# Down-projection of four FFN tiles: one product of 8 x 22 weight blocks, or seven products of half tiles

## The chip, the cores and the metric

The kernel runs as one program on all 8 cores of one Trainium2 chip, two dies of four cores. Each core handles one prompt sequence (2048 tokens and 16 meta tokens) and 16 of the 128 sample tokens. There is no exchange between cores. The metric is the device time in microseconds (us) of the slowest core, as a median over runs.

Names of engines: TensorE is PE in the profile (its weight loads are PEld), VectorE is DVE, ScalarE is ACT, GpSimd is POOL, SyncE is SP. SP and POOL issue the DMAs. SBUF is the on-chip memory, PSUM the accumulators that PE writes: 8 banks of 512 fp32 columns.

## The reference, cut to what matters

```python
def trunk_layer(x, ...):                       # x: (B, T, 1024)
    h = rmsnorm(x, g_pre_mix); z = h @ w_in    # token mixer: pooling and short convolution, two gates
    ...
    x = x + rmsnorm(merged @ w_o, g_post_mix)
    h = rmsnorm(x, g_pre_ffn)
    upc, new_ffn = causal_dwconv(h @ w_up, buf_ffn, w_ffn_conv)   # (B, T, 2*2816), width 3
    gate, val = jnp.split(upc, 2, axis=-1)
    y = (jax.nn.silu(gate) * val) @ w_down                        # (B, T, 2816) @ (2816, 1024)
    x = x + rmsnorm(y, g_post_ffn)
```

The outputs are the rows after the layer and the last rows of the pooling, convolution and FFN inputs, for prompts and samples. The change touches the product with w_down.

## The kernel before

The work is feature-major: a tile is 128 channels (partitions) by up to 512 tokens, and products are PE matmuls with a 128x128 weight block as the stationary operand and N tokens as the moving one, in bf16, summed in a PSUM bank.

The 2080 tokens go through two phases. The mixer phase has 5 tiles (512 tokens, then 392 four times). In each, `F_block` makes 16 input projections with pooling and convolution on DVE, `B` makes the gates and the merge, `WO` the output projection, and `epi` the norms, the residual (x is added by a POOL-issued DMA that accumulates into SBUF) and the FFN input, which goes through DRAM (`h2T`). The FFN phase has 5 tiles of `TB_N` = 448, 456, 448, 456 and 256 tokens. In each, `pair(t, j)` for j = 0 to 21 makes one gate and one value chunk of 128 channels: 2 x 8 matmuls into two PSUM banks, a copy with the first convolution tap on ACT (L879), two more taps for both on DVE (L883, four instructions), silu on ACT (L896), and the product on POOL (L897) into row j of the gated activation G (22 rows of N tokens, bf16).

`wdown(t, m)` is the down-projection of tile t for 128 output channels m = 0 to 7: 22 matmuls of N columns in one bank, one per row of G. ACT then writes the result to Y, scaled (L914), and its square to YSQ (L917). The eight of tile t stand between the pairs of tile t+1, at the positions of `WD`, `WD1` and `WDL`. `epi_y(t)` sums the squares, has PE add them over the channels (one f32r matmul), takes the reciprocal root on ACT, scales Y on DVE (L931, four instructions of two rows each) and sends it with an accumulating POOL DMA onto the residual in `yT`. For the fourth tile POOL adds the residual itself (L936), in the last microseconds, and SP stores. The fifth tile's down-projection, `down_last`, is token-major: G is stationary, the weights move, in 66 matmuls of 512 and 44 of 256 columns; DVE and ACT normalize (L987, L982, L1000, L1002, L1006), SP stores `y_last`.

The fp32 weights w_dn are cast to bf16 by POOL DMAs during tiles 0 and 1 of the FFN (`wdn_load`), kept in DRAM as `w_dnb` and loaded again for each later tile: one load of 704 KB per m, into a ring of 4 buffers. A load is issued once the product that used its buffer is done. The last tile's weights need four more buffers.

Nothing is ordered by hand inside an engine but PE: `Sched` takes the operations in program order, keeps PE's order except for a few floating ones (the f32r sums), and lists the others by readiness and priority in its own model (`order`). Each engine then works strictly down its list, waiting for semaphores; a waiting instruction holds all behind it. The seven PSUM banks 0 to 6 are given out in turn (`next_bank`), so a matmul group also waits until ACT and DVE are done with what stood in its bank seven groups before.

## Time and profile before

| | |
|---|---|
| Median of 3 runs | 807.48 us (806.51 to 807.51) |
| Span of the profiled execution, slowest core (2) | 812.6 us; all cores 803.4 to 812.6 us |
| PE busy | 798.6 us, 98%, 4500 matmuls |
| DVE, ACT, POOL busy | 551.9 us (68%), 447.8 us (55%), 255.3 us (31%) |
| DMA | 107 MB, mean 132 GB/s |

The profile is of one execution. Its page gives no time for it beyond the spans: the slowest core's 812.6 us is its own time, 0.6% over the median of the timed runs, and its other die stands at 803.5 us. Busy is the time an engine has at least one instruction in work, so two that overlap count once; the mean of one instruction can therefore be larger than busy divided by count. The page cuts the span into 40 slices, names for each group of instructions its busy time, its idle time before them and what ended that, and follows a chain of work back from the end. An engine that idles off that chain costs nothing.

### The profile page before, as it was taken

The page shows a single profiled execution, that of the slowest core. Times are in us where ns is not written, and L with a number is a line of the kernel's source. Part 1 is how long each engine was busy: PE and PEld are TensorE (multiplying, and loading weights), DVE is VectorE, ACT ScalarE, POOL GpSimd, SP SyncE. Part 2 cuts the span into 40 slices and gives each one's busy share as a digit, 9 for nine tenths or more (in the row PEclk, how much of TensorE's full clock was granted, in tenths as well). Part 3 has the DMA queues.
Part 4 walks back from the last instruction along what each step waited for, and adds up shares of the span by engine and source line. Part 5 has one row for each costly group of instructions (what it writes and reads, how often), then busy time and mean ns, then how long its engine had stood idle before and what let it go on. Part 6 is the DMA issues. An engine that isn't in the chain of part 4 may idle for free.

```text
span 812.6 us, 15177 instructions; the slowest of 8 cores (803.4 to 812.6 us)
## 1 busy us (share of the span) xinstructions
PE 798.6 (98%) x4500; PEld 438.4 (54%) x4500; DVE 551.9 (68%) x990; ACT 447.8 (55%) x1012; POOL 255.3 (31%) x268
## 2 busy tenths in 40 slices
PE   7999999999999999999999999999999999999997
PEld 5444455555555555554545555555555555576764
DVE  3897448896986785677989553766557655576566
ACT  3433284675565644586676444745447444576553
POOL 5542002001201144489534322342223422233124
PEclk9999999999999999999999999999999999999999
DMA  9999805856215989998972874472223722249736
GB/s 181 200 164 155 158 4 116 186 141 133 70 41 122 188 140 196 160 157 122 180 184 47 131 146 131 102 137 79 72 72 71 133 95 72 73 84 228 269 109 219
DMA packets 76543, 107.00 MB, mean 132 GB/s; under 512 B 12432, under 2 KB 65808, under 8 KB 76448
## 3 DMA queue, kind: packets, MB, share of 16 engines
q0 software_dynamic: 38992, 43.11, 37.9%
q1 hardware_dynamic: 37472, 62.94, 25.6%
q8 instruction: 38, 0.62, 0.3%
q14 instruction: 41, 0.34, 0.1%
HBM read 107.34 MB, written 29.03 MB: 168 GB/s over the span
## 4 chain that ended last, share of the span: by engine, by line
PE 92%; DMA 3%; DVE 2%; issue 2%; ACT 1%; DVEq 0%; ACTq 0%; POOLq 0%; POOL 0%
PE ps L510 92%; DMA big<-xT 2%; DMA big<-w_in 1%; DVE big L597 0%; DVE big L765 0%; DVE big L767 0%; DVE big L761 0%; ACT L568 0%; DVEq L1200 0%; DVE big L654 0%; ACT big L1079 0%; ACT big L568 0%; DVE big L660 0%; ACT big L748 0%; DVE big L706 0%
## 5 line engine op out<-in xcount | busy, mean ns | idle before, releaser
L510 PE MATMUL ps<-big 128*128 128x392 bf16 (+7 forms) x4482 | 798.0, 341 | 8.8 <-ACT big L1058 2.0
L510 PEld LDWEIGHTS ps<-big 128*128 128x128 bf16 x4482 | 435.0, 98 | 367.2 <-issue 16.2
L883 DVE SCALAR_TENSOR_TENSOR big<-ps,big 128x456 f32<-128x456 f32 (+2 forms) x440 | 253.4, 636 | 125.2 <-ACT big L876 108.8
L897 POOL TENSOR_TENSOR big<-big 128x448 bf16<-128x448 f32 (+2 forms) x110 | 119.0, 1084 | 263.4 <-ACT big L896 185.2
L879 ACT ACTIVATE big<-ps,big 128x448 f32<-128x448 f32 (+2 forms) x220 | 126.7, 598 | 18.6 <-PE ps L510 11.5
L896 ACT ACTIVATE big<-big 128x448 f32<-128x448 f32 (+2 forms) x110 | 59.9, 545 | 45.9 <-DVE big L883 44.0
L748 ACT ACTIVATE big<-ps 128x392 f32<-128x392 f32 (+1 forms) x80 | 39.2, 514 | 57.7 <-PE ps L510 29.1
L873 ACT ACTIVATE ps<-big 128x4 f32<-128x4 f32 (+1 forms) x100 | 17.6, 176 | 94.5 <-PE ps L510 94.1
L521 POOL DMA_DIRECT2D big<-xT x16 | 14.9, 958 | 164.5 <-DVE big L808 104.3
L523 POOL DMA_DIRECT2D big<-w_up x44 | 32.5, 756 | 54.3 <-PE ps L510 49.4
L761 DVE SCALAR_TENSOR_TENSOR big<-ps,big 128x392 f32<-128x392 f32 (+1 forms) x40 | 25.8, 645 | 31.5 <-PE ps L510 31.4
L556 DVE TENSOR_TENSOR big<-big 128x1568 bf16<-128x1568 bf16 (+3 forms) x28 | 23.5, 846 | 28.5 <-ACT big L780 22.5
L654 DVE TENSOR_TENSOR big<-big 128x406 f32<-128x406 f32 (+7 forms) x50 | 29.8, 597 | 1.7 <-ACT big L720 0.7
L523 POOL DMA_DIRECT2D big<-w_in x32 | 23.2, 756 | 21.8 <-DMA big<-w_in 10.5
L778 ACT ACTIVATE big<-ps,big 128x392 f32<-128x392 f32 (+1 forms) x40 | 24.2, 611 | 10.3 <-PE ps L510 9.6
L597 DVE SCALAR_TENSOR_TENSOR big<-big 128x392 bf16<-128x392 f32 (+1 forms) x40 | 24.4, 646 | 6.8 <-ACT big L574 6.8
L914 ACT ACTIVATE big<-ps,big 128x448 f32<-128x448 f32 (+1 forms) x32 | 20.4, 637 | 14.9 <-PE ps L510 13.7
L623 ACT ACTIVATE big<-big 128x392 f32<-128x392 f32 (+1 forms) x20 | 12.7, 638 | 28.6 <-DVE big L712 28.4
L626 DVE SCALAR_TENSOR_TENSOR big<-big 128x392 f32<-128x392 f32 (+1 forms) x40 | 25.5, 642 | 3.2 <-ACT big L623 2.9
L832 DVE SCALAR_TENSOR_TENSOR big<-big 128x392 bf16<-128x392 f32 (+1 forms) x40 | 25.6, 687 | 2.1 <-ACT big L571 1.9
L767 DVE TENSOR_TENSOR big<-big 128x392 bf16<-128x392 f32 (+1 forms) x40 | 24.9, 631 | 2.9 <-DVE big L765 0.9
L765 DVE TENSOR_TENSOR big<-ps,big 128x392 f32<-128x392 f32 (+1 forms) x40 | 23.4, 584 | 1.2
(74 smaller groups left out, 394.7 us busy)
## 6 DMA issues: line engine op xcount, KB each, us to landing
big<-w_dnb SPq DMA_DIRECT2D x32, 704.0 KB, 5.0
big<-w_up POOLq DMA_DIRECT2D x44, 256.0 KB, 14.8
big<-w_in POOLq DMA_DIRECT2D x32, 256.0 KB, 22.1
big<-xT POOLq DMA_DIRECT2D x16, 392.0 KB, 7.8
big<-w_dn POOLq DMA_DIRECT2D x8, 704.0 KB, 10.8
w_dnb<-big SPq DMA_DIRECT2D x8, 704.0 KB, 5.7
big<-xT SPq DMA_DIRECT2D x6, 784.0 KB, 6.0
yT<-big SPq DMA_DIRECT2D x6, 784.0 KB, 7.1
```

What stands on the lines that cost most here:

```text
L510: ins = e.matmul(o, lhsT=l, rhs=x, start=(start and i == 0), stop=(stop and i == last))
L523: return S.add("pool", lambda e: e.dma_start(out=out, in_=in_, max_dma_last_dim=mx), r, w, dma=True, byts=byts, pri=pri, after=after)
L626: dve(lambda e, k=k: e.scalar_tensor_tensor(out=cv, in0=p[:, 2 + k + lo:2 + k + N], scalar=cc(C_WC + 4 * k + c), in1=cv, op0=ALU.mult, op1 ...
L654: dve(lambda e, nx=nx, cur=cur, s=s, a2=a2: e.tensor_tensor(out=nx[:, a2:W], in0=cur[:, a2:W], in1=cur[:, a2 - s:W - s], op=ALU.add), [ct] ...
L748: act(lambda e, b=b, g=g: e.activation(out=GT[t].ap[:, g, lo:N], in_=bank(b, N, lo), func=AF.Sigmoid), [("ps", b)], [GT[t].t(g, 1)], N, ps ...
L761: dve(lambda e: e.scalar_tensor_tensor(out=A_, in0=bank(bp, N, lo), scalar=cc(C_PS + m), in1=A_, op0=ALU.mult, op1=ALU.mult), [("ps", bp), ...
L767: dve(lambda e: e.tensor_tensor(out=MERGED[t].ap[:, m, lo:N], in0=A_, in1=B_, op=ALU.add), [G_.t(ga, 1), G_.t(gb, 1)], [MERGED[t].t(m, 1)], N)
L832: dve(lambda e: e.scalar_tensor_tensor(out=h, in0=r, scalar=cc(C_G3 + k), in1=SD.ap[:, rs, lo:N], op0=ALU.mult, op1=ALU.mult), [R[t].t(k, ...
L879: act(lambda e, b=b, fj=fj, tt=tt: e.activation(out=tt[:, 0:n], in_=bank(b, n), func=AF.Copy, scale=cc(C_WF + fj)), [("ps", b), KCST], [to ...
L883: dve(lambda e, b=b, fj=fj, tt=tt, k=k: e.scalar_tensor_tensor(out=tt[:, 0:n], in0=ps[:, b * 512 + k:b * 512 + k + n], scalar=cc(C_WF + 44 ...
L896: act(lambda e: e.activation(out=g, in_=g, func=AF.Silu), [T.t(0, 1)], [T.t(0, 1)], N, tab="silu")
L897: S.add("pool", lambda e: e.tensor_tensor(out=gb.ap[:, j, 0:N], in0=g, in1=v, op=ALU.mult), [T.t()], [gb.t(j, 1)], dur=N * 2.17 + 100)
```

## The change

For tiles 0 to 3 the product of w_down (8 x 22 blocks) with G (22 rows of N tokens) is split in two along output channels (m 0 to 3 and 4 to 7), along the inner dimension (FFN channels 0 to 10 and 11 to 21) and along tokens (N/2 and N/2), and made by Strassen's seven products A to G of 4 x 11 blocks with 11 rows of N/2. Each product is two steps (`md` 0 and 1) of 2 x 11 matmuls of N/2 columns in one bank: 14 steps per tile instead of 8, each 22 matmuls. `sumb` makes the five sums of quarters of G in bf16: on DVE (A, B, C, D, E: 11 rows of N/2), and for tile 3 C, D and E on POOL in pieces of up to 4 rows. `put` (ACT) writes a bank to a quarter of Y and `acc` (DVE) adds it to one or subtracts it, 8 and 16 instructions per tile. G's rows are interleaved by `JORD` so that a half of the inner dimension is every second row.

The five weight sums are made once, in the mixer phase. All of w_dn is cast by 8 POOL DMAs from DRAM to DRAM in `B(0)`. `prep`, called 16 times between `B(1)` and the last mixer tile, loads four 3-block pieces by two SP DMAs, makes five sums in three DVE instructions and stores them by two SP DMAs to `w_dns`. Steps load half-matrices of 704 KB for two m, from `w_dns` or `w_dnb`, through a ring of 3 buffers. The last tile's eight whole loads (`wlast_load`) stay, four of them into the ring's area: one after step 5, three as the ring ends.

`epi_y` scales row by row with the gain g4 (8 instructions instead of 4). The convolution's sample columns of the last tile move out of `pair` (44 small DVE instructions) into `sample_cols`, four DVE and one ACT instruction at the end. The temporary buffers TB of `pair` are 3 throughout instead of 5 from tile 2 on. Tile widths become 448, 464, 448, 448, 256; some mixer buffers lie elsewhere in SBUF.

```diff
-TB_N = (448, 456, 448, 456, 256)
-OB = (0, 448, 904, 1352, 1808)
+TB_N = (448, 464, 448, 448, 256)
+OB = (0, 448, 912, 1360, 1808)
...
-NB = 456
+NB = 464
+FH = FC // 2
+HW = FH * 128
+JORD = [j for i in range(FH) for j in (i, FH + i)]
...
+    w_dns = nc.dram_tensor("w_dns", [5, 4, 128, HW], BF16).ap()
...
-    NR = 4
+    NR = 3
...
+    Y3 = Buf(W0, KC, TB_N[3])
+    W_DNX = [Buf(Y3.end + DW * i, 1, FC * 128, True) for i in range(4)]
...
+    YB = [Y, Y, Y, Y3]
...
-    TB.append(bl(2, NB))
-    TB.append(bl(2, NB))
-    assert bl.o <= XSQ2[4].end
...
+    SA = Buf(XSQ2[4].end - FH * NB // 4, FH, NB // 2, True)
+    XTR = [Buf(R[4].end, 1, NBL)] * 4 + [Buf(YSQ.off + NBL * i, 1, NBL) for i in range(4)]
...
+    SB5 = Buf(W_DN[3].off, FH, NB // 2, True)
...
+    def prep():
+        for h in range(2):
+            sp_dma(pi.ap[:, 2 * h:2 * h + 2, 0:w],
+                   w_dnb[m + 4 * h].rearrange("p (h c) -> p h c", h=2)[:, :, 128 * c:128 * c + w], [("wdb", m + 4 * h)],
+                   [pi.t(2 * h, 2)], 128 * 2 * w * 2, after=[last_pe[0]])
+        pin = pi.ap[:, :, 0:w].rearrange("p (a b) c -> p a b c", b=2)
+        k = [pi.t(j, 1) for j in range(4)]
+        for o, i0, i1, op, wt, f in ((po.ap[:, 0:2, 0:w], pi.ap[:, 0:2, 0:w], pi.ap[:, 2:4, 0:w], ALU.subtract, [po.t(0, 2)], 2),
+                                     (po.ap[:, 2, 0:w], pi.ap[:, 0, 0:w], pi.ap[:, 3, 0:w], ALU.add, [po.t(2, 1)], 1),
+                                     (pin[:, :, 0, :], pin[:, :, 0, :], pin[:, :, 1, :], ALU.add, [k[0], k[2]], 2)):
+            dve(lambda e, o=o, i0=i0, i1=i1, op=op: e.tensor_tensor(out=o, in0=i0, in1=i1, op=op), k, wt, f * w, rate=2.0,
+                pri=-20000.0)
+        dst = w_dns[:, m, :, 128 * c:128 * c + w].rearrange("v p c -> p v c")
+        sp_dma(dst[:, 0:3, :], po.ap[:, :, 0:w], [po.t()], [("wds", m, c, 0)], 128 * 3 * w * 2, pri=-200000.0)
+        sp_dma(dst[:, 3:5, :], pin[:, :, 0, :], [k[0], k[2]], [("wds", m, c, 1)], 128 * 2 * w * 2, pri=-200000.0)
+
+    STEPS = [(p, md) for p in "ABCDEFG" for md in range(2)]
+    WSRC = {"A": 2, "B": 1, "E": 0, "F": 4, "G": 3}
...
+    def sw_load(s):
+        p, md = STEPS[s % len(STEPS)]
+        buf = W_DN[s % NR]
+        dst = buf.flat.rearrange("p (m c) -> p m c", m=2)
+        if p in WSRC:
+            src = w_dns[WSRC[p], 2 * md:2 * md + 2]
         else:
+            h = 4 if p == "C" else 0
+            o = HW if p == "C" else 0
+            src = w_dnb[h + 2 * md:h + 2 * md + 2, :, o:o + HW]
+        sp_dma(dst, src.rearrange("m p c -> p m c"), dep, [buf.t()], 128 * 2 * HW * 2, after=[last_pe[0]])
+
+    def wlast_load(m):
+        buf = W_DN[m] if m < 4 else W_DNX[m - 4]
+        sp_dma(buf.flat, w_dnb[m], [("wdb", m)], [buf.t()], 128 * FC * 128 * 2, after=[last_pe[0]])
...
-        T = TB[set_rr[0] % (3 if t < 2 else 5)]
+        T = TB[set_rr[0] % 3]
...
-                dve(lambda e, b=b, fj=fj, tt=tt: e.scalar_tensor_tensor(
-                    out=tt[:, n:N], in0=ps[:, b * 512 + 2 + n:b * 512 + N + 2], scalar=cc(C_WF + 88 + fj),
-                    in1=PRE.ap[:, fj, :], op0=ALU.mult, op1=ALU.add), [("ps", b), PRE.t(), KCST], [tok], NS, stt=True)
...
+    def sample_cols():
+        dve(lambda e: e.tensor_tensor(out=S44, in0=tl, in1=w2, op=ALU.mult), tk + [KCST], [TB[0].t()], 704)
+        dve(lambda e: e.tensor_tensor(out=S44, in0=S44, in1=pr, op=ALU.add), [TB[0].t(), PRE.t()], [TB[0].t()], 704)
+        act(lambda e: e.activation(out=S44[:, 0], in_=S44[:, 0], func=AF.Silu), [TB[0].t(0, 1)], [TB[0].t(0, 1)], 352, tab="silu")
+        for i in range(2):
+            dve(lambda e, i=i: e.tensor_tensor(out=gb.ap.rearrange("p (j i) n -> p i j n", i=2)[:, i, :, N - NS:N],
+                                               in0=S44[:, 0, FH * i:FH * i + FH], in1=S44[:, 1, FH * i:FH * i + FH], op=ALU.mult),
+                [TB[0].t()], [("sb", gb.off + (2 * j + i) * gb.cw + (N - NS) // 2, NS // 2) for j in range(FH)], 176)
+
...
+    def gap(t, par, half):
+        gb, h = G[t % 2], TB_N[t] // 2
+        return gb.ap.rearrange("p (i two) n -> p i two n", two=2)[:, :, par, half * h:half * h + h]
...
+        (p0, h0), (p1, h1), op, o = {
+            "A": ((0, 0), (1, 1), ALU.add, SA), "B": ((1, 0), (1, 1), ALU.add, SB5),
+            "C": ((1, 0), (0, 0), ALU.subtract, (1, 0)), "D": ((1, 1), (0, 1), ALU.subtract, SA),
+            "E": ((0, 0), (0, 1), ALU.add, (0, 1))}[which]
+        out, wt = (gap(t, *o), gtok(t, *o)) if isinstance(o, tuple) else (o.ap[:, :, 0:h], [o.t()])
+        if t == NTB - 2 and which in "CDE":
+            for i in range(0, FH, 4):
+                pool_tt(lambda e, i=i, k=min(FH, i + 4): e.tensor_tensor(out=out[:, i:k, :], in0=gap(t, p0, h0)[:, i:k, :],
+                                                       in1=gap(t, p1, h1)[:, i:k, :], op=op),
...
+        dve(lambda e: e.tensor_tensor(out=out, in0=gap(t, p0, h0), in1=gap(t, p1, h1), op=op),
+            gtok(t, p0, h0) + gtok(t, p1, h1), wt, FH * h, rate=2.0)
+
+    RHS = {"A": SA, "B": SB5, "C": (1, 0), "D": SA, "E": (0, 1), "F": (0, 0), "G": (1, 1)}
...
+        p, md = STEPS[i]
+        wt = W_DN[s % NR]
+        wb = wt.flat.rearrange("p (m k c) -> p m k c", m=2, k=FH)
+        r = RHS[p]
+        rhs, rt = (gap(t, *r), gtok(t, *r)) if isinstance(r, tuple) else (r.ap[:, :, 0:h], [r.t()])
...
-        for k0, k1 in ((0, FC),):
-            pe([(bank(b, N), wb[:, k, :], gb.ap[:, k, 0:N]) for k in range(k0, k1)], [wt.t(), gb.t(k0, k1 - k0)],
-               [("ps", b)], N, start=k0 == 0, stop=k1 == FC)
-        act(lambda e: e.activation(out=Y.ap[:, m, 0:N], in_=bank(b, N), func=AF.Copy, scale=cc(C_G4 + m)),
-            [("ps", b), KCST], [Y.t(m, 1)], N, psum=True, ap=1)
-        r = m if m < 2 else 2 + m % 2
-        act(lambda e: e.activation(out=YSQ.ap[:, r, 0:N], in_=bank(b, N), func=AF.Square), [("ps", b)], [YSQ.t(r, 1)], N,
+        for mi in range(2):
+            pe([(bank(b, mi * h + h, mi * h), wb[:, mi, k, :], rhs[:, k, :]) for k in range(FH)], [wt.t()] + rt, [("ps", b)], h,
+               start=True, stop=True)
+        if s + NR < NST:
+            sw_load(s + NR)
...
+            act(lambda e: e.activation(out=o, in_=src, func=AF.Copy, scale=scale), [("ps", b)], tk, N, psum=True)
+            dve(lambda e: e.tensor_tensor(out=o, in0=o, in1=src, op=op), [("ps", b)] + tk, tk, N)
+        if p == "A":
+            put(4, 1)
+            put(0, 0)
+        elif p == "B":
+            acc(0, 0, ALU.add)
+        elif p == "C":
+            put(4, 0)
+            acc(0, 0, ALU.add)
+        elif p == "D":
+            put(0, 1, -1.0)
+            acc(4, 1, ALU.subtract)
+        elif p == "E":
+            acc(4, 1, ALU.subtract)
+        elif p == "F":
+            acc(4, 0, ALU.add)
+            acc(4, 1, ALU.subtract)
+        else:
+            acc(0, 0, ALU.subtract)
+            acc(0, 1, ALU.add)
+        if p in "FG":
...
+            act(lambda e: e.activation(out=YSQ.ap[:, r0:r0 + 2, 0:N], in_=YB[t].ap[:, m0:m0 + 2, 0:N], func=AF.Square),
+                [YB[t].t(m0, 2)], [YSQ.t(r0, 2)], 2 * N)
...
-        for q in range(4):
-            dve(lambda e, q=q: e.tensor_tensor(out=Y.ap[:, 2 * q:2 * q + 2, 0:N], in0=Y.ap[:, 2 * q:2 * q + 2, 0:N],
-                                               in1=sdb, op=ALU.mult),
-                [Y.t(2 * q, 2), ("ps", SB)], [Y.t(2 * q, 2)], 2 * N)
+        for q in (0, 2, 1, 3):
+            for m in (2 * q, 2 * q + 1):
+                dve(lambda e, m=m: e.scalar_tensor_tensor(out=YB[t].ap[:, m, 0:N], in0=YB[t].ap[:, m, 0:N], scalar=cc(C_G4 + m),
+                                                          in1=bank(SB, N), op0=ALU.mult, op1=ALU.mult),
+                    [YB[t].t(m, 1), ("ps", SB), KCST], [YB[t].t(m, 1)], N, stt=True, pri=-12000.0)
...
+            if t == 0:
+                r = m // 2 + 4 * (m % 2)
+                pool_dma(w_dnb[r], w_dn[r], [], [("wdb", r)], 128 * FC * 128 * 4, mx=2048, after=[last_pe[0]])
+            if t == 1 and m % 2 == 0:
+                for _ in range(2):
+                    prep()
...
+    pre_ffn()
+    for _ in range(8):
+        prep()
...
-    WD = {5: 0, 7: 1, 10: 2, 12: 3, 14: 4, 16: 5, 19: 6, 21: 7}
-    WD1 = {9: 0, 11: 1, 13: 2, 15: 3, 17: 4, 19: 5, 20: 6, 21: 7}
-    WDL = {3: 0, 5: 1, 7: 2, 10: 3, 12: 4, 14: 5, 16: 6, 19: 7}
+    WD = (6, 8, 9, 10, 11, 12, 13, 14, 15, 16, 18, 19, 20, 21)
+    WDL = (4, 5, 6, 8, 9, 10, 11, 13, 14, 15, 16, 18, 19, 20)
...
+            if t == 0 and j in (12, 14, 16):
+                sw_load((j - 12) // 2)
+            if t == NTB - 1 and j in (7, 10, 12, 17):
+                wlast_load(4 + (7, 10, 12, 17).index(j))
...
-            wd = WD1 if t == 1 else WDL if t == NTB - 1 else WD
-            if t > 0 and j in wd:
-                wdown(t - 1, wd[j])
+            for i in [i for i, x in enumerate(WDL if t == NTB - 1 else WD) if t > 0 and x == j]:
+                if i == 0:
+                    sumb(t - 1, "A")
+                wdown(t - 1, i)
+                if i in (0, 1, 2, 4):
+                    sumb(t - 1, {0: "B", 1: "C", 2: "D", 4: "E"}[i])
+                if t == NTB - 1 and i == 5:
+                    wlast_load(3)
+                if t == NTB - 1 and i > 10:
+                    wlast_load((len(STEPS) * (t - 1) + i) % NR)
...
+    sample_cols()
...
-    for j in range(FC):
+    for j in JORD:
...
```

How the lists of the engines change at three places. First PE at the start of FFN tile 2, whose pairs are 448 columns wide, with tile 1's down-projection between them (456 columns before, 232 after) and the f32r sum of tile 0. Before:

```order
L510 MATMUL ps<-big 128x448 x54
L510 MATMUL ps<-f32r 128x448
L510 MATMUL ps<-big 128x448 x64
L510 MATMUL ps<-big 128x456 x22
L510 MATMUL ps<-big 128x448 x32
L510 MATMUL ps<-big 128x456 x22
L510 MATMUL ps<-big 128x448 x48
L510 MATMUL ps<-big 128x456 x22
```

After:

```order
L569 MATMUL ps<-big 128x448 x64
L569 MATMUL ps<-f32r 128x448
L569 MATMUL ps<-big 128x448 x48
L569 MATMUL ps<-big 128x232 x22
L569 MATMUL ps<-big 128x448 x32
L569 MATMUL ps<-big 128x232 x22
L569 MATMUL ps<-big 128x448 x16
L569 MATMUL ps<-big 128x232 x22
L569 MATMUL ps<-big 128x448 x16
L569 MATMUL ps<-big 128x232 x22
```

The f32r sum stands after four pairs (64 matmuls) instead of two, the first step after seven pairs instead of six, and the steps of 22 short matmuls follow one or two pairs apart instead of two or three. (The first row of before also holds tile 0's last 22.)

DVE at the same place, from the end of tile 1's pairs. L883 and L943 are the convolution taps before and after; L931 and L1067 scale Y of tile 0; L559 and L618 feed the f32r sum; L920 and L1056 add squares; L996 is `sumb` of tile 1. Before:

```order
L920 TENSOR_TENSOR big<-big 128x2x448
L559 TENSOR_TENSOR f32r<-big 128x448
L883 SCALAR_TENSOR_TENSOR big<-ps,big 128x448 x8
L931 TENSOR_TENSOR big<-big,ps 128x2x448
L883 SCALAR_TENSOR_TENSOR big<-ps,big 128x448 x4
L931 TENSOR_TENSOR big<-big,ps 128x2x448
L883 SCALAR_TENSOR_TENSOR big<-ps,big 128x448 x12
L931 TENSOR_TENSOR big<-big,ps 128x2x448 x2
L883 SCALAR_TENSOR_TENSOR big<-ps,big 128x448 x28
```

After:

```order
L996 TENSOR_TENSOR big<-big 128x2552
L1056 TENSOR_TENSOR big<-big 128x2x448
L943 SCALAR_TENSOR_TENSOR big<-ps,big 128x448 x8
L618 TENSOR_TENSOR f32r<-big 128x448
L943 SCALAR_TENSOR_TENSOR big<-ps,big 128x448 x4
L996 TENSOR_TENSOR big<-big 128x2552
L943 SCALAR_TENSOR_TENSOR big<-ps,big 128x448 x4
L996 TENSOR_TENSOR big<-big 128x11x232
L1067 SCALAR_TENSOR_TENSOR big<-big,ps 128x448 x4
L943 SCALAR_TENSOR_TENSOR big<-ps,big 128x448
L1067 SCALAR_TENSOR_TENSOR big<-big,ps 128x448 x4
L943 SCALAR_TENSOR_TENSOR big<-ps,big 128x448 x19
```

Sum A stands ahead of the first taps of tile 2, B and C between the taps of its first pairs, and the eight scalings of Y stand nearly together instead of spread over six pairs.

PE at the end of the program: the last down-projection steps of tile 3 (456 or 224 columns), the last pairs (256 columns), `down_last` (512 and 256 columns) and tile 3's f32r sum. Before:

```order
L510 MATMUL ps<-big 128x456 x22
L510 MATMUL ps<-big 128x256 x48
L510 MATMUL ps<-big 128x456 x22
L510 MATMUL ps<-big 128x256 x32
L510 MATMUL ps<-big 128x512 x20
L510 MATMUL ps<-f32r 128x456
L510 MATMUL ps<-big 128x512 x46
L510 MATMUL ps<-big 128x256 x44
```

After:

```order
L569 MATMUL ps<-big 128x224 x22
L569 MATMUL ps<-big 128x256 x16
L569 MATMUL ps<-big 128x224 x22
L569 MATMUL ps<-big 128x256 x16
L569 MATMUL ps<-big 128x512 x44
L569 MATMUL ps<-f32r 128x448
L569 MATMUL ps<-big 128x512 x22
L569 MATMUL ps<-big 128x256 x44
```

The f32r sum moves from 90 matmuls before the end to 66 before it, and one pair instead of two stands behind the last step.

## Rows read from the trace of the kernel before

**Rows 1.** Engines of the whole span: busy us, share, instructions.

```profile
span 812.6 us, 15177 instructions; the slowest of 8 cores (803.4 to 812.6 us)
...
PE 798.6 (98%) x4500; PEld 438.4 (54%) x4500; DVE 551.9 (68%) x990; ACT 447.8 (55%) x1012; POOL 255.3 (31%) x268
```

**Rows 2.** The chain of waits, share of the span by engine.

```profile
PE 92%; DMA 3%; DVE 2%; issue 2%; ACT 1%; DVEq 0%; ACTq 0%; POOLq 0%; POOL 0%
```

**Rows 3.** Spans and granted clock of the two dies.

```profile
die 0 (median of its cores): 811.4 us, clock 0.989
die 1 (median of its cores): 803.5 us, clock 0.999
```

**Rows 4.** PE by shape: count | busy us, mean ns | idle before.

```profile
L510 PE MATMUL ps<-big 128*128 128x456 bf16 x1056 | 210.1, 357 | 0.0
L510 PE MATMUL ps<-big 128*128 128x448 bf16 x704 | 138.0, 354 | 0.0
...
L510 PE MATMUL ps<-big 128*128 128x256 bf16 x396 | 45.0, 272 | 0.0
```

**Rows 5.** PE weight loads by shape, same columns.

```profile
L510 PEld LDWEIGHTS ps<-big 128*128 128x128 bf16 x4482 | 435.0, 98 | 367.2 <-issue 16.2
```

**Rows 6.** PE by shape from 6 to 12 us.

```profile
L510 PE MATMUL ps<-big 128*128 128x128 bf16 x53 | 3.4, 219 | 0.0
```

**Rows 7.** DVE by shape, whole span.

```profile
L883 DVE SCALAR_TENSOR_TENSOR big<-ps,big 128x448 f32<-128x448 f32 x176 | 108.0, 677 | 49.9 <-ACT big L876 49.6
...
L931 DVE TENSOR_TENSOR big<-big,ps 128x896 f32<-128x896 f32 x8 | 8.6, 1080 | 2.2 <-ACT ps L571 2.2
...
L556 DVE TENSOR_TENSOR big<-big 128x784 bf16<-128x784 bf16 x12 | 6.7, 560 | 0.3
...
L712 DVE TENSOR_TENSOR big<-ps,big 128x392 f32<-128x392 f32 x16 | 9.0, 561 | 2.3 <-PE ps L510 1.9 <-ACT big L676 0.4
...
L556 DVE TENSOR_TENSOR big<-big 128x2048 bf16<-128x2048 bf16 x2 | 2.4, 1223 | 9.5 <-ACT big L780 9.5
```

**Rows 8.** Stretches: busy us (count) by engine, PE clock, DMA share, GB/s.

```profile
170.00:330.00 160.00, 158.50 (x951) 93.09 (x950) 124.96 (x232) 90.66 (x169) 37.16 (x44) 0.99 0.66 133
230.00:240.00 10.00, 10.00 (x62) 5.92 (x61) 9.12 (x18) 6.77 (x17) 0.00 (x0) 1.00 0.11 27
310.00:320.00 10.00, 8.50 (x52) 4.83 (x51) 4.65 (x9) 3.37 (x6) 2.87 (x4) 1.00 1.10 163
722.00:790.00 68.00, 68.00 (x481) 46.48 (x479) 43.33 (x125) 42.94 (x141) 18.78 (x23) 1.00 0.71 182
```

**Rows 9.** Chain in order of time, 295 to 320 us: start, us, what.

```profile
304.36 10.47 DMA big<-xT
```

**Rows 10.** Loads from w_dnb, 500 to 720 us.

```profile
DMA to landing us min/median/max: 4.5/4.8/6.0
```

**Rows 11.** Loads from w_dnb, 722 to 800 us.

```profile
DMA to landing us min/median/max: 4.6/9.8/12.8
```

**Rows 12.** DMA issues from 715 to 792 us: count, KB, us to landing.

```profile
big<-w_dnb SPq DMA_DIRECT2D x13, 704.0 KB, 9.5
```

**Rows 13.** yT transfers from 490 us: us to landing.

```profile
DMA to landing us min/median/max: 2.9/8.1/17.8
```

**Rows 14.** Timeline of the end: start us, us, engine, line, what.

```profile
791.74 0.56 PE L510 MATMUL ps<-f32r 128*128 128x456 f32 x1
...
792.14 15.20 PE L510 MATMUL ps<-big 128*128 128x512 bf16 x90
...
797.09 9.25 POOL L936 TENSOR_TENSOR big<-big 128x912 f32<-128x912 f32 x4 [4.90 <-DVE big L931]
...
800.50 3.86 DVE L1006 SCALAR_TENSOR_TENSOR big<-big 128x512 f32<-128x512 f32 x2
...
808.70 1.42 DVE L1006 SCALAR_TENSOR_TENSOR big<-big 128x512 f32<-128x512 f32 x2 [0.26 <-ACT big L1002]
```

164 lines of the change are left out of this document (97 added, 67 removed).

## The prediction, made before the changed kernel ran

> **What bounds the kernel now.** I read the page's engine lines and its chain of waits first, then the spans of the cores, then PE by shape of matmul, then stretches of the stages that the change touches, and last the transfers and the timeline of the end. The reader is to see in the first two that PE is busy 798.6 us of 812.6 [rows 1] and holds 92% of the chain [rows 2]; PE's forms have no idle time before them in the FFN shapes [rows 4]. So the time is the number of matmuls times what each takes, plus start and tail. DVE is at 68% and not on the chain. The profiled execution has one die at a granted clock of 0.989 and 811.4 us, the other at 0.999 and 803.5 us [rows 3]. My durations are from core 2 of the first die; its span, 812.6 us, is 5.1 us (0.6%) over the median of 807.5. I work out a difference against that span and take it from the median; at 0.6% of a few microseconds the clock makes no odds.
>
> **PE, what goes and what comes.** A matmul of 448 columns takes 138.0 us / 704 = 196.0 ns, one of 456 takes 199.0 ns, one of 256 takes 113.6 ns [rows 4]. The slope is (199.0 - 113.6) / 200 = 0.427 ns a column, so I estimate 99.9 ns for 224 columns and 103.4 ns for 232, with about 4.3 ns that do not depend on width. The trace has no matmul of that width with changing weights. Removed: four tiles of 176, 352 x 196.0 + 352 x 199.0 ns = 139.0 us. Added: 56 steps of 22, 924 x 99.9 + 308 x 103.4 ns = 124.2 us. Gain 14.9 us. The columns fall by one eighth, and the fixed part eats some of it, having 528 more matmuls. The pairs' total width does not change. Bounds of this term: with the fixed part at nothing the gain is 17.0 us (39,776 columns by slope); with the 256-column duration for each short matmul it is 139.0 - 1232 x 113.6 ns = -0.9 us. I take the line through two shapes, since 128-column matmuls already ran at 64 ns (3.4 us / 53, from 6 to 12 us [rows 6]), under the line's 59 + 5.
>
> Each short matmul needs its own weight load, and the loads last 98 ns on average [rows 5], as long as the new matmul. In the 6 to 12 us stretch matmuls with their loads follow each other every 64 ns [rows 6], so the loads overlap each other and do not set the pace; I add nothing. The Trainium skill (TensorE: Matmul & The Clock Gate, LDWEIGHTS) gives a load as its columns over 1.2 GHz, 107 ns for 128. Were that an interval and not a latency, 1232 matmuls would each take some 7 ns more and 8.7 us of the gain would go; by that rule the 64 ns could not be, so the trace speaks against it.
>
> **DVE in the FFN.** A tile of 448 had 88 taps at 108.0 / 176 = 0.614 us, 4 scalings at 1.08 us and four sums of squares at some 0.6 us [rows 7]: 61 us. Added are 16 additions from PSUM, at 0.56 us for 392 columns [rows 7] and so about 0.62; five sums of 2464 bf16, at 1.22 us for 2048 [rows 7] and so about 1.47; and 8 scalings at 0.68 instead of 4 at 1.08. That is 9.9 + 7.4 + 1.1 = 18.4 us, in a tile whose PE time is now 352 x 196.0 + 308 x 99.9 ns = 99.8 us: 80% busy. PE ran without a gap from 230 to 240 us with DVE at 9.12 of 10 [rows 8], and seven banks hold three pairs, so I cost it at nothing but for waits at places, below. ACT's 16 instructions per tile become 12, some wider: nothing.
>
> The sums of G stand in DVE's list ahead of taps, sum A even ahead of the first taps of the tile, where it waits for POOL's last product. Behind it wait the taps of the first pair, and behind them PE for a bank. Between the last pair and the first step PE has seven pairs of 3.1 us (tiles 1 to 3), or five of 1.8 us and a step (tile 4). Cost 0 to 1 us each time, I take 0.5 us for the narrow tile and, together with steps that find Y not yet sent (the yT transfers take 8.1 us, at most 17.8 [rows 13], and step 1 now writes rows that all four of them read, where the second product before wrote only row 1), 0.5 us for the others. Bounds 0 and 4 us.
>
> **DVE and DMA in the mixer.** 16 preparations of three instructions, about 0.55 + 0.36 + 0.55 us by the widths next to 0.56 us for 784 and 1.22 for 2048 [rows 7], are 22 us of DVE between some 170 and 330 us, where it is busy 124.96 of 160 us, 78% [rows 8]. It becomes 92%. They are listed with priority, so they push evacuations back by up to 1.5 us at a time. Cover: the banks. Bounds 0 and 6 us; I take 1.0 us. Their 13 MB of transfers and the 17 MB of the casts in `B(0)` find a DMA share of 0.66 there. One place has no slack: PE idles 1.5 us between 310 and 320 us [rows 8], and the chain there goes through an xT transfer of 10.47 us that starts at 304.36 [rows 9]. The last preparations' transfers fall just ahead of it. Bounds -1.5 and +4 us, taken +1.0. In return the casts no longer run in FFN tiles 0 and 1, where PE did not wait for them: no gain.
>
> **The last tile's weights.** Ring loads (704 KB) are issued as a step ends and needed three steps later, with three gaps between: at least 2 x 2.2 us of steps and 3 pairs of 16 x 113.6 ns = 1.82 us, 9.9 us; on average (16 pairs in 13 gaps) 11.1 us. In tiles 1 to 3 it is 4.4 + 3 x 3.1 = 13.8 us at least, against landings of 4.5 to 6.0 us [rows 10]: no wait. In the last tile landings were 4.6 to 12.8, median 9.8 us [rows 11], harmless with a ring of four whose steps of 4.4 us stood two or three pairs apart. Now 19 loads (11 of the ring, 8 whole) stand where 13 did [rows 12], at a DMA share of 0.71 [rows 8]. A load that lands after L us stretches a ring's period to (L + 2.2) / 3 per step, from 4.4 us. L = 12.8 adds 0.56 x 11 = 6.2 us, L = 9.8 nothing. I take 1.8 us, bounds 0 and 12. After the last step only one pair and 22 matmuls of 512 columns (1.8 + 4.8 = 6.6 us) hide the last whole load, where two pairs and the same did (8.4 us): 0.7 us, bounds 0 and 5.
>
> **The end.** Before, tile 3's f32r sum ran at 791.74; POOL's four residual additions end at 797.09 + 9.25 = 806.34, 14.6 us later; PE ends at 792.14 + 15.20 = 807.3, and the span 5.3 us after that with `y_last` [rows 1, 14]. Now the sum stands 66 matmuls before the end, 22 x 216 + 44 x 109 ns + 0.5 = 10.1 us. POOL then ends 4.5 us after PE, and the store lands at least 2.9 us later [rows 13]: 7.4 instead of 5.3 us, +2.1. The final normalization also runs beside POOL's additions, where two L1006 took 3.86 us and not 1.42 [rows 14], which only makes both branches end together. I take +2.2, bounds +1 and +5. `sample_cols` (three microseconds of DVE and ACT) has the 9.5 us of the first 44 matmuls as cover, and 44 small DVE instructions leave the pairs.
>
> **The sum.** -14.9 + 2.2 + 0.7 + 1.8 + 1.0 (xT) + 1.0 (mixer DVE) + 1.0 (tile entries and Y) = -7.2 us. The profiled 812.6 would be 805.4, the median 807.5 becomes 800.3.
>
> **Rivals.**
> 1. The covers hold. Only the tail shows: 807.5 - 14.9 + 2.2 = 794.8. For it: PE waited 0.0 us in the FFN shapes [rows 4] and ran full beside a DVE at 91%. Against: the last tile's landings.
> 2. DVE becomes the bound in places. Four or five preparations (5.8 us) meet a 10 us stretch that has 0.9 us free, in several mixer tiles, and PE runs out of banks: 5 us more, 805.3. For it: DVE's 92% in 160 us. Against: DVE's work there is uneven and most of it is not waited for at once. The Trainium skill (SBUF — State Buffer, Who interferes with whom) says that a DVE instruction with two SBUF inputs and a reading POOL instruction exclude each other whole. The trace agrees in that L1006 takes 1.93 beside POOL's additions and 0.71 alone. By it each of the 17 DVE sums could wait for a product of POOL, which would feed this rival.
> 3. Slower: the last tile is bound by its weights. Loads grow from 13 to 19, and if landings grow with them, 9.8 x 19 / 13 = 14.3 us, the period is 5.5 us a step, 1.1 x 11 = 12 us instead of my 1.8: 810.4. It decides from L = 13.6 us on, where the gain is gone. For it: 12.8 us was already seen. Against: the median is pushed up by queued loads that nobody waits for; a ring paces itself.
> 4. The short matmuls are slower than the line, paced by their weight loads: at 107 ns 809.0, at the 256-column duration higher. Against: 64 ns for 128 columns.
>
> **Chances.** Forecast 0.42 (its own range 797 to 804), first rival 0.28, second 0.13, third 0.12, fourth 0.03, anything else 0.02. The 8-in-10 range runs from 793.8, just below the first rival, to 809.0, short of the third's centre. A measurement of this kernel tells about 0.2%, 1.6 us, from no change. Faster than 805.9: 0.42 + 0.28 and two thirds of the second, 0.79. Within: 0.07. Slower: 0.14, the third and most of the fourth.
>
> **What would show it.** PE should have 1232 matmuls of 224 and 232 columns at about 100 ns busy each (124 us); 107 or more makes the fourth rival right. Idle before PE in the last tile, ended by w_dns or w_dnb transfers with landings of 10 us and more, is the ring term: under 1 us for the first rival, 10 or more for the third. PE idle behind DVE between 170 and 330 us is the second. The f32r sum should stand some 10 us before PE's end and the span end over 7 us after it. I am wrong in the main if PE's idle time in the middle of the program grows beyond 10 us or not at all.

## The result, and the profile after

| | before | after |
|---|---|---|
| Median | 807.5 us (4 runs, 806.5 to 808.1) | 854.3 us (3 runs, 853.3 to 856.3) |
| Ratio | | 1.0585, 95% interval 1.0564 to 1.0606: 47 us slower |
| Span of the profiled execution | 812.6 us | 852.7 us |

Executions in which one die ran at a lower clock than the other (one more of the kernel after, with 959.8 us, and some of the runs below) are left out of the times, and where a run has hardly any other, the undisturbed die alone is compared.

The prediction said 800.3 us and 0.79 for faster. It is wrong in sign, and outside its range of 793.8 to 809.0. The page of the kernel after, its head, its engine line and the chain's shares, beside [rows 1, 2]:

```profile
span 852.7 us, 16749 instructions; the slowest of 8 cores (843.0 to 852.7 us)
...
PE 790.2 (93%) x5028; PEld 489.2 (57%) x5028; DVE 626.4 (73%) x1095; ACT 443.4 (52%) x998; POOL 274.0 (32%) x277
...
PE 66%; DMA 22%; DVE 4%; issue 3%; POOL 2%; ACT 1%; SPq 1%; DVEq 0%; ACTq 0%; POOLq 0%
```

PE is busy for less time (790.2 against 798.6 us) and is idle for 62.5 us where it was idle for 14.0. DMA holds 22% of the chain, before 3%. Stretches of the kernel after (busy us and count of PE, PEld, DVE, ACT, POOL, then PE clock, DMA share, GB/s):

```profile
100.00:120.00 20.00, 10.83 (x52) 4.85 (x50) 3.81 (x6) 3.33 (x5) 1.33 (x2) 0.83 1.05 159
120.00:140.00 20.00, 17.08 (x85) 8.92 (x86) 10.03 (x17) 15.34 (x27) 0.00 (x0) 0.83 1.05 111
140.00:160.00 20.00, 12.00 (x72) 6.85 (x70) 3.71 (x7) 5.85 (x8) 0.00 (x0) 0.86 0.80 151
160.00:200.00 40.00, 34.65 (x181) 19.25 (x182) 33.30 (x61) 19.40 (x37) 4.40 (x4) 0.86 0.66 162
...
320.00:360.00 40.00, 29.11 (x163) 15.81 (x161) 22.50 (x52) 11.78 (x21) 15.52 (x18) 0.95 0.74 143
...
480.00:775.00 295.00, 293.47 (x2107) 203.23 (x2106) 232.05 (x379) 164.49 (x416) 101.26 (x84) 1.00 0.51 143
775.00:853.00 78.00, 60.32 (x487) 47.93 (x485) 48.56 (x97) 31.84 (x102) 25.44 (x23) 0.92 0.78 232
```

Three places lose: 100 to 200 us (25 us idle), 320 to 360 us (11 us), and the last tile. Between them the FFN runs nearly full. After each gap the granted clock of the stretch is a mix of its levels of 1.2 and 2.4 GHz (0.83 and 0.86 of full), so a gap costs more than its idle time.

The starts of the matmuls in the traces cut PE's time into stages, in us. The figures are medians over cores: all eight, but cores 4 to 7 for the kernel before and a_nosums, and 0 to 3 for b_room and t3_noprep. "FFN" goes from the first matmul of tile 0's pairs to the first of the last tile's, "last tile" to the start of `down_last`. The lower rows are the experiments below.

| | mixer | FFN | last tile | `down_last` | after PE | span |
|---|---|---|---|---|---|---|
| before | 334.2 | 370.3 | 72.5 | 19.7 | 5.4 | 803.5 |
| after | 377.0 | 361.7 | 78.5 | 19.4 | 10.7 | 849.5 |
| b_casts | 356.5 | 370.3 | 72.5 | 19.7 | 5.2 | 825.8 |
| b_room | 335.4 | 371.6 | 72.5 | 19.7 | 5.2 | 805.9 |
| s_noprep | 357.1 | 361.7 | 80.8 | 19.4 | 11.3 | 831.5 |
| a_nosums | 366.2 | 362.0 | 81.8 | 19.4 | 11.2 | 840.8 |
| s_room | 336.6 | 361.7 | 82.2 | 19.4 | 11.4 | 813.1 |
| s_room_noload | 337.1 | 361.7 | 68.5 | 19.4 | 10.9 | 799.3 |
| t3_noprep | 335.4 | 361.8 | 76.2 | 21.2 | 5.3 | 802.0 |

So the kernel after loses 43 us in the mixer, gains 8.6 in the FFN, and loses 6 in the last tile and 5 at the end. The time of a run is that of its slowest core, and cores differ more where PE waits (843.0 to 852.7 us after, 803.4 to 803.8 on cores 4 to 7 before), so differences of times come out somewhat larger than those of this table.

PE's largest waits (us in total, times, longest) and PE by shape:

```profile
PE ps L569 <- DVE f32r L618: 15.1, 2, 12.1
PE ps L569 <- DVE big L820: 10.8, 2, 10.4
PE ps L569 <- DMA big<-w_dns: 6.8, 3, 4.7
```

```profile
L569 PE MATMUL ps<-big 128*128 128x224 bf16 x924 | 97.4, 262 | 6.8 <-DMA big<-w_dns 6.8
...
L569 PE MATMUL ps<-big 128*128 128x232 bf16 x308 | 32.8, 263 | 0.0
```

These rows give the new matmuls 130.2 us where the removed ones had 139.0. They can't be set against each other, since a busy time by shape counts the overlap at each change of shape twice: by the profile each group of 22 ends with a matmul that lasts 260 ns (224 columns) or 357 (456), while the next group has begun. The part on the prediction has what a matmul takes. A wait "behind DVE" is not yet a cause: the chain in order of time (start, us, what) says what DVE waited for.

```profile
93.98 23.14 DMA big<-xT
...
139.69 21.07 DMA big<-w_dnb
160.85 0.10 DVE big L506
...
171.10 15.04 DMA big<-xT
```

The load of the next tile's x takes 23 us, a preparation's 192 KB take 21 us while its sum L506 holds DVE's list, and the residual's addition takes 15 us. The first two stand beside the eight casts (issued at 75.5 to 103.0 us, landing up to 61.7 us later); the third stands beside stores of the preparations and of the residual. The issues of the casts (KB each, us to landing):

```profile
w_dnb<-w_dn POOLq DMA_DIRECT2D x8, 704.0 KB, 40.9
```

### The profile page after: what moved, and what is told of

Read it like the earlier page. It is cut to its first block, busy times and chain, and to the rows that moved or that the text cites. A ratio compares the mean times of both kernels' runs of the same rounds, so it can differ in the third digit from the quotient of the medians.

```text
span 852.7 us, 16749 instructions; the slowest of 8 cores (843.0 to 852.7 us)
## 1 busy us (share of the span) xinstructions
PE 790.2 (93%) x5028; PEld 489.2 (57%) x5028; DVE 626.4 (73%) x1095; ACT 443.4 (52%) x998; POOL 274.0 (32%) x277
## 4 chain that ended last, share of the span: by engine, by line
PE 66%; DMA 22%; DVE 4%; issue 3%; POOL 2%; ACT 1%; SPq 1%; DVEq 0%; ACTq 0%; POOLq 0%
PE ps L569 66%; DMA big<-xT 6%; DMA big<-w_in 6%; DMA big<-w_dnb 3%; DMA big<-w_o 3%; DMA big<-w_dns 2%; DMA w_dns<-big 2%; POOL big L582 1%; SPq L576 1%; POOL big L790 1%; DVE big L867 1%; DVE big L1067 0%; DVE big L685 0%; DVE big L506 0%; DVE big L826 0%
## 5 line engine op out<-in xcount | busy, mean ns | idle before, releaser
L569 PE MATMUL ps<-big 128*128 128x392 bf16 (+9 forms) x5010 | 788.7, 320 | 36.9 <-DVE big L820 10.8
L569 PEld LDWEIGHTS ps<-big 128*128 128x128 bf16 x5010 | 485.6, 99 | 335.6 <-issue 61.2
L943 DVE SCALAR_TENSOR_TENSOR big<-ps,big 128x448 f32<-128x448 f32 (+2 forms) x440 | 251.0, 634 | 74.5 <-ACT big L936 64.6
L953 POOL TENSOR_TENSOR big<-big 128x448 bf16<-128x448 f32 (+2 forms) x110 | 125.8, 1145 | 248.2 <-ACT big L952 160.1
L506 DVE TENSOR_TENSOR big<-big 128x768 bf16<-128x768 bf16 (+3 forms) x48 | 24.6, 525 | 31.7 <-DMA big<-w_dnb 31.0
L1029 DVE TENSOR_TENSOR big<-big,ps 128x448 f32<-128x448 f32 (+1 forms) x64 | 38.0, 614 | 8.7 <-PE ps L569 8.1
L820 DVE SCALAR_TENSOR_TENSOR big<-ps,big 128x392 f32<-128x392 f32 (+1 forms) x40 | 25.7, 642 | 20.1 <-PE ps L569 18.8
L682 ACT ACTIVATE big<-big 128x392 f32<-128x392 f32 (+1 forms) x20 | 12.7, 637 | 38.6 <-DVE big L771 38.5
L713 DVE TENSOR_TENSOR big<-big 128x406 f32<-128x406 f32 (+7 forms) x50 | 29.6, 594 | 0.8
L656 DVE SCALAR_TENSOR_TENSOR big<-big 128x392 bf16<-128x392 f32 (+1 forms) x40 | 24.4, 644 | 7.9 <-ACT big L633 7.9
L996 DVE TENSOR_TENSOR big<-big 128x2464 bf16<-128x2464 bf16 (+1 forms) x17 | 27.3, 1604 | 0.3
L875 ACT ACTIVATE big<-big 128x784 bf16<-128x784 f32 (+1 forms) x20 | 17.8, 892 | 17.9 <-DMA big<-xT 17.3
```

What stands on the lines that cost most here:

```text
L569: ins = e.matmul(o, lhsT=l, rhs=x, start=(start and i == 0), stop=(stop and i == last))
L713: dve(lambda e, nx=nx, cur=cur, s=s, a2=a2: e.tensor_tensor(out=nx[:, a2:W], in0=cur[:, a2:W], in1=cur[:, a2 - s:W - s], op=ALU.add), [ct] ...
L820: dve(lambda e: e.scalar_tensor_tensor(out=A_, in0=bank(bp, N, lo), scalar=cc(C_PS + m), in1=A_, op0=ALU.mult, op1=ALU.mult), [("ps", bp), ...
L943: dve(lambda e, b=b, fj=fj, tt=tt, k=k: e.scalar_tensor_tensor(out=tt[:, 0:n], in0=ps[:, b * 512 + k:b * 512 + k + n], scalar=cc(C_WF + 44 ...
L953: S.add("pool", lambda e: e.tensor_tensor(out=gb.ap[:, q, 0:n], in0=g, in1=v, op=ALU.mult), [T.t()], [("sb", gb.off + q * gb.cw, n // 2)], ...
L996: dve(lambda e: e.tensor_tensor(out=out, in0=gap(t, p0, h0), in1=gap(t, p1, h1), op=op), gtok(t, p0, h0) + gtok(t, p1, h1), wt, FH * h, ra ...
```

## The experiments

Thirteen kernels, each against the kernel before in runs on the same chip. Names with b_ start from the kernel before, the others from the kernel after.

### What the casts cost, and where

**b_casts**, edit on the kernel before:

```diff
             if t == L:
                 wup(2)
+            if t == 0:
+                r = m // 2 + 4 * (m % 2)
+                pool_dma(w_dnx[r], w_dn[r], [], [("wdx", r)], 128 * FC * 128 * 4, mx=2048, after=[last_pe[0]])
```

> The kernel before, with only the eight casts of w_dn (fp32, DRAM) to a spare bf16 tensor in DRAM added in B(0), one per m, at the place where the changed kernel has them; nothing reads them. Theory CAST (the casts take the DMA engines and the loads of X[2] and of the residual land late, whoever waits): PE idles 12 to 20 us between 100 and 160 us, the loads of xT there land in about 20 us instead of 6, and the time is 820 to 828 us. Theory SUMS (only the DVE sums that stand in the list and wait for their pieces stop the rest): 807 to 810 us, PE idle under 2 us there.

Measured: 831.9 us against 807.0, ratio 1.031 (1.0287 to 1.0332), 25 us more from eight DMAs that nobody waits for; the mixer is 22 us longer on the median core. Two stretches and, of the chain, the load that PE's wait goes back to:

```profile
100.00:120.00 20.00, 9.37 (x45) 4.17 (x43) 3.08 (x5) 1.60 (x2) 1.33 (x2) 0.81 1.04 151
120.00:140.00 20.00, 12.25 (x53) 5.88 (x54) 5.08 (x8) 14.85 (x25) 0.00 (x0) 0.68 1.05 113
```

```profile
93.00 30.50 DMA big<-xT
```

No weight sum stands in DVE's list here, so CAST holds for about half of the loss, and is larger than expected (over the 828 us of its range). What one cast takes, from the queue that carries POOL's DMAs (packets, MB, share of 16 engines), first the kernel before, then b_casts:

```profile
q0 software_dynamic: 38992, 43.11, 37.9%
```

```profile
q0 software_dynamic: 44752, 48.87, 43.0%
```

0.430 x 829.6 - 0.379 x 812.6 = 48.7 us of all 16 engines, 6.1 us for a cast of 1.4 MB into 0.7 MB; the same eight casts give 45.7 us in b_gap and 47.2 in b_room. This is time of packets, which grows and shrinks with what stands beside them: the same 62.94 MB on SP's queue took 208 us before and 197 in b_casts. So it is good to some 10 us in 50.

**b_gap** and **b_room**: the same edit with the casts at other places.

```diff
-            if t == 0: ...
+    b_gap:  CAST = {("b",2,4), ("b",2,6), ("f",3,0), ("f",3,2), ("f",3,4), ("f",3,6), ("f",3,8), ("f",3,10)}
+    b_room: CAST = {("w",0,0), ("w",0,4), ("f",2,12), ("w",1,4), ("b",2,4), ("f",3,0), ("f",3,6), ("f",3,12)}
```

(b is B(t) after merge m, f is F_block i of tile t, w is WO(t) after row m.)

> The kernel before with the same eight casts to a spare tensor, now issued between 197 and 227 us (two in B(2), six in the F_blocks of tile 3), where the trace of before has a DMA share of 0.26 and no load that PE waits for soon. Theory PLACE (a cast costs only what lands late beside it): 807 to 809 us. Theory VOLUME (17 MB more in the mixer cost time wherever they stand): 815 us or more, with PE idle between 200 and 300 us.

> The kernel before with the same eight casts, now spaced at 8 us and more, which is over the 6.1 us of all 16 DMA engines that one cast takes (48.8 us for eight, from the queue shares of b_casts and before), and kept off the 8 us ahead of the residual's additions: two in WO(0), one in F_block 12 of tile 2, one in WO(1), one in B(2), three in the F_blocks of tile 3. Theory ROOM (casts cost nothing where the engines have the time and nothing waited for lands beside them): 807 to 809 us. Rival (any cast in the mixer costs, as landings of all transfers beside it double): 812 to 818 us, 0.6 to 1.3 us a cast.

Measured: b_gap 823.1 us, ratio 1.0177 (1.0153 to 1.0202). VOLUME has the numbers (815 us or more, PE idle between 200 and 300 us), but not the reason, as b_room shows below. 14.5 us are lost, at one place. Eight casts 3.4 us apart need 6.1 us each, so their backlog reached the additions of the residual (chain: start, us, what, and the stretch):

```profile
250.97 23.64 DMA big<-xT
```

```profile
240.00:280.00 40.00, 26.02 (x149) 14.71 (x147) 16.49 (x27) 14.98 (x26) 3.54 (x4) 0.83 0.99 136
```

b_room: 818.2 us against 817.3 for the kernel before on that chip, whose second die is slower with either kernel. On the first die the slowest core has 807.0 against 805.9 us (medians of 11 and 17 executions). About 1 us. 818.2 alone would be the rival's number; against the kernel before on the same chip ROOM holds: the same bytes, in the mixer, cost 25 us, 14.5 us or next to nothing by what stands beside them.

### What the preparations cost

**s_noprep** and **a_nosums**:

```diff
 s_noprep:
-            src = w_dns[WSRC[p], 2 * md:2 * md + 2]
+            src = w_dnb[h + 2 * md:h + 2 * md + 2, :, 0:HW]
-    for _ in range(8):
-        prep()
 a_nosums:
-        for o, i0, i1, op, wt, f in (...): dve(... tensor_tensor ...)
-        sp_dma(dst[:, 0:3, :], po.ap[:, :, 0:w], ...)
+        sp_dma(dst[:, 0:3, :], pi.ap[:, 0:3, 0:w], ...)
```

> The changed kernel without the 16 preparations: the steps that read w_dns load a half of w_dnb of the same size instead, so the weight sums are left out and the products are of other numbers. The casts stay in B(0). Theory CAST: the first stall stays (12 to 20 us), those behind the sums (10.4 and 12.1 us of waits, and 11 us at 320 to 360) go: about 825 us, between 820 and 832. Theory SUMS: 807 to 812 us, since all of the mixer's loss goes. If neither, and the loss is in the FFN: above 845 us.

> The changed kernel with casts and all transfers of the preparations where they were, but without the 48 DVE sums: the loaded pieces are stored as they are, so the weight sums are left out. Theory SUMS (of the 18 us that the preparations cost, 855 against 837, the most comes from DVE sums that wait in DVE's list): 835 to 840 us. Theory TRANSFERS (the 13.8 MB that they load and store delay others): 849 to 856 us.

Measured: s_noprep 837.1 us, ratio 1.0365 (1.0346 to 1.0385), 18 us below the kernel after by the ratios, and 5 us over CAST's range. a_nosums: ratio 1.0494 (1.0464 to 1.0524), from two executions at 848.1 and 848.5 us, just under TRANSFERS' range. So the preparations cost 18 us, of which by the ratios the sums are 7 and the 13 MB of transfers 10 to 11, each to 3 us. By the table's mixer the sums are 11 and the transfers 9. That is about half each, and neither theory holds alone. In a_nosums (core 4) PE is full at 140 to 160 us and nearly so at 320 to 360, so these two gaps of the kernel after were the sums':

```profile
140.00:160.00 20.00, 20.00 (x122) 11.76 (x121) 15.93 (x27) 8.51 (x15) 4.38 (x4) 1.00 1.03 178
160.00:200.00 40.00, 26.54 (x141) 14.58 (x139) 20.77 (x39) 17.78 (x33) 0.00 (x0) 0.87 0.69 163
320.00:360.00 40.00, 39.25 (x237) 22.95 (x236) 31.05 (x66) 19.08 (x32) 19.65 (x25) 1.00 1.03 179
```

The gap before 200 us is larger without the sums. It is not the preparations' alone: on the same core s_noprep, which has none, is idle for 5.3 of those 40 us.

The SP queue's shares, first in the kernel after, then in s_noprep, give the transfers' engine time:

```profile
q1 hardware_dynamic: 67552, 93.16, 36.0%
```

```profile
q1 hardware_dynamic: 48096, 80.17, 32.2%
```

That is 0.360 x 852.7 - 0.322 x 835.7 = 37.9 us (POOL's queue had 10 us less beside them, so it may be 28). With the casts that is 87 us, or 77. What the kernel before had to give, with the stretch of the casts first:

```profile
70.00:100.00 30.00, 30.00 (x144) 13.97 (x143) 15.19 (x24) 8.65 (x17) 0.71 (x1) 1.00 0.94 156
100.00:120.00 20.00, 20.00 (x103) 9.97 (x102) 8.98 (x14) 16.71 (x28) 0.00 (x0) 1.00 0.05 19
120.00:140.00 20.00, 20.00 (x122) 11.77 (x121) 16.74 (x28) 9.00 (x15) 3.35 (x3) 1.00 0.44 104
140.00:160.00 20.00, 20.00 (x115) 11.44 (x113) 15.17 (x29) 12.30 (x21) 1.08 (x1) 0.93 0.97 207
160.00:200.00 40.00, 40.00 (x243) 23.54 (x241) 33.02 (x59) 26.68 (x51) 3.48 (x4) 1.00 0.50 117
200.00:240.00 40.00, 40.00 (x238) 23.41 (x237) 35.76 (x61) 23.43 (x50) 4.74 (x3) 0.98 0.26 79
240.00:280.00 40.00, 40.00 (x243) 23.58 (x242) 30.51 (x58) 24.56 (x43) 7.11 (x9) 1.00 0.70 137
280.00:320.00 40.00, 38.50 (x233) 22.50 (x232) 27.00 (x57) 17.30 (x32) 16.64 (x20) 1.00 0.91 158
```

One minus the DMA share, times the length, summed from 100 to 320 us: 19.0 + 11.2 + 0.6 + 20.0 + 29.6 + 12.0 + 3.6 = 96 us. I take it that 77 to 87 of 96 us can't be placed without touching something that is waited for. The tries below fit that, but don't show it, as each also has sums or loads at places of its own.

### Tries to mend it

**s_spread** (casts one at a time from B(1) to B(2), no preparations), **s_repair** (the same with preparations spread over tiles 2 and 3), **s_late** (casts in FFN tile 0, no preparations):

```diff
 s_spread, s_repair:
+    CAST = {("b",1,0), ("b",1,3), ("b",1,6), ("f",2,2), ("f",2,6), ("f",2,10), ("f",2,14), ("b",2,2)}
 s_repair: sums of one preparation listed at the call of the next
+                dve(..., pri=-20000.0, after=[last_pe[0]])
 s_late:
+            if t == 0 and j in (1, 3, 4, 6, 7, 9, 10, 12):
+                pool_dma(w_dnb[r], w_dn[r], ...)
```

> As s_noprep (weight sums left out), and the eight casts issued one at a time between B(1) and B(2) instead of in B(0). This leaves the products, their loads and the end. Theory A (the mixer's stalls are all of the loss that is not in the last tile): the mixer takes its time of before to within 2 us; the products gain 8.8 us (139.0 to 130.2 us as the trace after has them), the last tile loses about 14 us and the end 3 to 5: 814 to 819 us. Theory B (the last tile's loss is the late clock and goes with the stalls): 800 to 804 us.

> The whole computation: casts spread as in s_spread, and the 16 preparations spread from the mixer tile 2 to 3, each with its DVE sums listed one call after its loads were issued, with two buffers in turn. If the stalls came from the place of the casts and from sums that wait for their pieces, it is within 3 us of s_spread: 814 to 821 us (theory A), 800 to 806 us (theory B). If the preparations' 22 us of DVE work and 13 MB themselves cost (rival 2 of the prediction), it is 5 us or more above s_spread, with PE waiting behind DVE between 160 and 300 us.

> The changed kernel without preparations (weight sums left out, steps read halves of w_dnb) and with the eight casts in FFN tile 0 instead of B(0). The mixer should take its time of before. Theory RING (the products gain 10.8 us by 103.0 and 107.1 ns a matmul at full clock, the last tile loses some 14 us to loads that land late and to the clock after them, the end 3 to 5): 812 to 817 us. If the last tile only lost because of what came before it: 800 to 804. If eight casts in tile 0 hold up the w_up loads there: over 820, with PE idle between 350 and 470 us.

None is a repair. s_spread: 831.4 us, ratio 1.0315 (1.0285 to 1.0344), outside both theories; its casts met the busiest stretch of the mixer (the row at 140 to 160 us above), and PE is idle for 12.7 us from 160 to 200 us. s_repair: 884.3 us, ratio 1.0951 (1.0901 to 1.1001), slower than the kernel after, so its last case ("5 us or more above s_spread") came true. A sum behind its load is not enough: the load waits for the buffer, the buffer for the stores, and DVE's list for all three (chain):

```profile
377.46 16.08 DMA w_dns<-big
...
394.24 11.39 DMA big<-w_dnb
405.73 0.06 DVE big L512
```

s_late: ratio 1.048 (1.044 to 1.052), from two executions. Its mixer is as before and it loses in tile 0, by its own third case, since the w_up loads go through POOL too:

```profile
PE ps L570 <- DMA big<-w_up: 25.0, 3, 15.9
```

**t3_noprep** and **t3_full** take the casts of b_room, make only three tiles by seven products, and the fourth as before; t3_full adds eight preparations at 210 to 330 us and eight in tile 0.

```diff
-    NST = len(STEPS) * (NTB - 1)
+    NST = len(STEPS) * (NTB - 2)
+            if t == NTB - 1 and j in WDL:
+                wdown_old(t - 1, WDL[j])
```

> Casts as in b_room; only the first three FFN tiles by seven products, the fourth, whose product is made in the last tile, as before with eight whole loads; no preparations (weight sums left out, steps read halves of w_dnb). Theory RING: the last tile is as before, the tail too, and three tiles gain 2.7 us each: 8 us below b_room, 799 to 802 us if b_room is at 808. Rival (the products lose by DVE or the ring in tiles 1 to 3 too): within 3 us of b_room.

> As t3_noprep with the weight sums: the whole computation. Eight preparations between 210 and 330 us, eight in FFN tile 0 in the ring's buffers, each sum listed one call after its loads. Theory ROOM: the 38 us of DMA time and 22 us of DVE time find room, at most 4 us above t3_noprep. Rival (the mixer and tile 0 have no room for them: DVE is at 80% in tile 0, and the w_up loads fill the DMA from 280 us on): 8 us or more above t3_noprep, no better than before.

t3_noprep: ratio 0.9974 (0.9943 to 1.0005), 2 us and not 8, and not clear of nothing. Its rival has the number (within 3 us of b_room) but not the reason: the three tiles gain the same 8.6 us as in the other kernels with the products. The loss is behind them. The last tile is 3.7 us longer than before, most of it at its entry, where the first product of the old kind waits for a row of Y that is still being sent, and `down_last` is 1.5 us longer, where PE waits for `sample_cols` (start, us, what, idle before):

```profile
722.73 56.52 PE L570 MATMUL ps<-big 128*128 128x256 bf16 x400 [3.01 <-ACT big L1075]
786.29 9.71 PE L570 MATMUL ps<-big 128*128 128x512 bf16 x66 [1.64 <-DVE big L970]
```

t3_full: ratio 1.0434 (1.0375 to 1.0492), some 37 us above t3_noprep; the rival holds. (It does all the work of the whole computation in its order, but its weight sums are not all right, so it is a time and no kernel to use.) It loses where the mixer ends and tile 0 begins, with DVE's taps behind sums that wait for their pieces:

```profile
360.00:400.00 40.00, 24.02 (x111) 11.37 (x109) 18.98 (x30) 12.43 (x26) 16.27 (x15) 0.78 1.08 185
```

### The products alone

**s_late_noload**, and then, without stalls elsewhere, **s_room** (casts of b_room, no preparations) and **s_room_noload**:

```diff
 both _noload:
-        if s + NR < NST:
+        if s + NR < NST - len(STEPS) + 3:
             sw_load(s + NR)
```

> As s_late, and eleven of the fourteen ring loads for the products of tile 3 (made in the last tile) left out: these steps use the weights that are in the ring. Theory RING: PE's wait for weights in the last tile goes and the clock with it, 13 us less than s_late, 799 to 804 us. Rival (the whole loads of the last tile and the end hold it): within 4 us of s_late.

> The changed kernel with the casts spaced as in b_room and without preparations (weight sums left out, steps read halves of w_dnb): the products alone. If the three parts add up (casts 25.4 us by b_casts, preparations 18 us by the changed kernel against s_noprep, the rest 4.7 us by s_noprep against b_casts), it is 4 to 7 us above the kernel before. If the products lose only because of the late clock and shifted transfers after the mixer's stalls, it is 5 us or more below it.

> As s_room, and eleven of the fourteen ring loads for the products of the last tile left out. Theory RING (the last tile's weights take what the products gain): 12 to 16 us below s_room, so 6 to 11 us below the kernel before. Rival (the end and the Y tile, not the weights): within 5 us of s_room.

Measured: s_late_noload 835.3 us, ratio 1.0334 (1.0309 to 1.036), 12 us below s_late by the ratios; the stall in tile 0 kept both far over the times expected. s_room 818.1 us, ratio 1.012 (1.010 to 1.014): the products cost 10 us, more than the 4 to 7 expected. s_room_noload: ratio 0.9943 (0.9926 to 0.996), 4.6 us faster than before, a little less than expected. The last tile's ring loads are 14.3 us, and 13.7 by the table. RING holds. PE in the last tile of s_room (start, us, [idle before <- releaser]), and the DMAs issued there from 738 to 770 us:

```profile
750.34 5.63 PE L570 MATMUL ps<-big 128*128 128x224 bf16 x38 [4.22 <-DMA big<-w_dnb]
...
767.96 28.17 PE L570 MATMUL ps<-big 128*128 128x224 bf16 x212 [4.84 <-DMA big<-w_dnb]
```

```profile
q1 hardware_dynamic: 1871, 5.95, 59.8%
q0 software_dynamic: 1088, 1.84, 39.0%
...
big<-w_dnb SPq DMA_DIRECT2D x5, 704.0 KB, 20.1
yT<-big POOLq DMA_DIRECT2D x4, 448.0 KB, 22.2
```

The five loads issued there take 20.1 us (median). The two queues fill the engines to 99%, with four accumulating transfers of Y that take 12.5 us of all engines for 1.84 MB. The same four transfers stood there in the kernel before, where the loads took 9.5 us [rows 12]; what is new is the number of loads. Without the eleven loads PE is full at the same place:

```profile
740.00:760.00 20.00, 20.00 (x197) 18.71 (x195) 12.60 (x30) 11.03 (x38) 7.95 (x10) 1.00 0.85 170
```

The end of the kernel after: the last f32r sum in the timeline, then of the chain PE's last work and the scaling behind it.

```profile
832.01 0.56 PE L569 MATMUL ps<-f32r 128*128 128x448 f32 x1
```

```profile
814.93 27.21 PE ps L569 x189
...
843.88 2.55 DVE big L1143
```

PE ends at 842.1 us and the span 10.6 us later, before 5.3 [rows 1, 14].

## Why the prediction was wrong

My own sign of being wrong in the main, over 10 us more of idle PE in the middle of the program, came true: 25 and 11 us in the mixer.

**The step that failed** is the sentence in "DVE and DMA in the mixer": "Their 13 MB of transfers and the 17 MB of the casts in `B(0)` find a DMA share of 0.66 there." That share is of 170 to 330 us [rows 8]. The casts are issued at 75 to 103 us, where the share was 0.94 already, and they were costed at nothing, without a bound. They cost 25 us (b_casts). The same sentence left the preparations' transfers at nothing but for the xT term: they cost 9 to 11 us (a_nosums against s_noprep). A mean share also hides that the free time lies in pieces. The chain had shown, at 304 us, that an xT transfer of 10.47 us stops PE [rows 9]. I took that for one place; every mixer tile has such transfers, the load of x and the additions, and beside the casts a load of x took 30.5 us (b_casts) and an addition 23.64 (b_gap).

**Mixer DVE**, +1.0 with bounds 0 and 6: the sums cost 7 to 11 us. The chain lays this not to the 22 us of work, as rival 2 had it, but to their place in the list ahead of what they wait for: 21.07 us at 139.69. No run has the work without the waits, so how much of it the work alone would cost is open.

**The xT transfer at 304 us**, +1.0 with bounds -1.5 and +4: part of the gap of 11 us at 320 to 360 us. It goes with the sums.

**PE's term**, -14.9: right. At full clock matmuls of 448 and 456 columns start 189 and 192 ns apart, those of 224 and 232 columns 96 and 99 ns (medians of all in the traces, each with a weight load of its own). So 352 x 189 + 352 x 192 = 134.1 us went and 924 x 96 + 308 x 99 = 119.2 us came: 14.9 us. That it fits to the tenth is luck. Both sides of my sum were 5 us too large, since I divided busy times by counts, and the rows of one window show the fault:

```profile
L569 PE MATMUL ps<-big 128*128 128x464 bf16 x153 | 31.4, 358 | 0.0
L569 PE MATMUL ps<-big 128*128 128x224 bf16 x198 | 20.4, 259 | 0.0
L569 PE MATMUL ps<-big 128*128 128x448 bf16 x60 | 11.5, 352 | 0.0
```

They are of 500 to 560 us in the kernel after and add up to 63.3 us in a window of 60. The 224-column matmuls, whose groups of 22 each end in a change of shape, look like 20.4 us / 198 = 103 ns. The same fault is in the 10.8 us that the expectation of s_late takes for the gain, in the 8.8 us of s_spread's, and in my own sign for rival 4: 130.2 us / 1232 is 106 ns by the rows, and yet the rival is false. Its price was off as well, since 107 instead of 99.9 and 103.4 ns is 7.7 us and not 8.7. The Trainium skill (TensorE: Matmul & The Clock Gate, LDWEIGHTS) gives a load as its columns over 1.2 GHz, 107 ns for 128; matmuls that start 96 ns apart, each with a load, lie under it, so here the loads do not set the pace.

**The last tile's weights**, +1.8 with bounds 0 and 12: 14.3 us (s_room against s_room_noload). In the kernel after, whose median core has 10.0 us, it is less. This is rival 3, which I gave 0.12. Its formula, (L + 2.2) / 3 a step, gives 7.4 instead of 4.4 us with L = 20.1 us, 15 us for five steps; as L and the five come from the same run, that agrees and tests nothing. L was wrong. I scaled it by the number of weight loads alone, and the share of 0.71 [rows 8] by nothing.

**The end**, +2.2 with bounds +1 and +5: 5.3 us. From the last f32r sum to the span's end it is 20.7 us, as before (20.9), and PE has 10.1 us left behind the sum, as I had it. What I had too short is the rest: the last scaling (L1143) runs until 848.1 us beside POOL's additions, and the last stores are issued at 847.5 to 849.5 us, while the additions end at 845.9.

**Tile entries and Y**, +1.0: 2.3 us. The columns alone would take 10.9 us off the FFN stage, and 8.6 went, in every kernel with the products in the table. With free weights the sum is -14.9 + 2.3 (entries) + 5.5 (end) + 2.9 (mixer with the casts of b_room, by the table) = -4.2 us; the table has -4.2 for s_room_noload and the times -4.6.

The parts by the times: casts 25, preparations 18, products with their last tile 10. That is 53 us where 47 are lost. By the table's stages they nearly add up: of 43 us in the mixer the casts are 22, the preparations 20; the rest is -8.6 in the FFN, +6.0 in the last tile, -0.3 and +5.3 at the end, 45 to 46 in all. The surplus of the times has two sources: each is that of the slowest core, and s_room's 10 us have 2.4 us of the spaced casts in them and a last tile that is 3.7 us longer than in the kernel after. Why the last tile loses less there was not separated.

## What to carry to other kernels

A transfer that nobody waits for is not free: price it in microseconds of all DMA engines, from a queue's share over the span, and set that against the free time of the stretch where it is issued, slice by slice. Then look for small transfers beside it that the bounding engine waits for, and multiply their landing by what it had already reached at a share of 1. Arithmetic that saves an eighth of the matmul columns in one layer (15 us here) can be paid only with traffic that fits into gaps; here it brought some 80 us of DMA engine time in the mixer and six more loads in the tile with the least room. And a sum listed with priority ahead of its data stops an engine for as long as the slowest store, load and sum in its buffer's circle. Last, take what a matmul costs from the starts of two in a row, not from a busy time by shape over a count: in groups of 22 the second was 7 ns too high for the short matmuls, and put the gain at 9 us where it is 15.

## What the runs showed of the hardware

- Matmuls of 128, 224, 256, 448 and 512 columns with a weight load each start 56, 96, 109, 189 and 216 ns apart (medians of both kernels), which is 0.417 ns a column and some 2.5 ns.
- A cast of 704 KB from DRAM to DRAM takes 5.7 to 6.1 us of all 16 engines (b_gap, b_room, b_casts), 118 GB/s written at 6.1. Transfers through the SP queue in the kernel before move 62.94 MB in 25.6% of 812.6 us, 303 GB/s.
- Queues share the engines rather than wait in turn: the x load on SP's queue took 30.5 us beside casts on POOL's, and a median of 7.0 us at the same place in the kernel before. From 94 to 123 us of b_casts POOL's queue had 83% of the engines' time and SP's 20%, by the profile's shares. The Trainium skill (DMA: Bandwidth & Descriptors, SWDGE vs HWDGE vs iDMA) says that each engine goes round between the two paths' queues; the trace agrees in that both moved at once.
- The accumulating transfers of Y on POOL's queue went at half the rate of SP's loads beside them: 12.5 us of all engines for 1.84 MB, 147 GB/s, against 19.1 us for 5.95 MB, 311 GB/s (s_room, 738 to 770 us). Their packets are half as large too (1.7 against 3.2 KB), so how much of it is the accumulation was not separated.
- Seen from PE, a gap of 10 us and more costs again afterwards: in b_casts the matmuls from 120 to 140 us ran at a granted clock of 0.68, with 12.25 us of busy time for 53, where 122 in the next 20 us had the full clock.
